# The router before the experts: last attention slab by token halves, logits as a plain f32 product of transposed x, choice on unscaled logits, first expert begun on half of its rows

## The reference, cut to what matters

```python
x = x + memory_cross_attention(rms_norm(x, xa_norm_g[i]), mem_n, xa_wq[i], xa_wkv[i], xa_wo[i])
h = rms_norm(x, ffn_norm_g[i])
...
logits = (t @ router_w).astype(jnp.float32)          # t = h, (256, 1024); router_w (1024, 8)
top_v, top_i = lax.top_k(logits, TOP_K)              # 2 of 8
top_w = jax.nn.softmax(top_v, axis=-1)
gates = jnp.sum(jax.nn.one_hot(top_i, N_EXPERTS) * top_w[..., None], axis=1)
for e in range(N_EXPERTS):
    out = out + gates[:, e:e + 1] * swiglu(t, w_gate[e], w_up[e], w_down[e])
```

## Time and profile before

| | us |
|---|---|
| median of 3 runs | 1642.45 |
| lowest and highest | 1641.81, 1644.15 |
| the profiled execution | 1642.63 |
| its span, first to last instruction | 1640.7 |

### The profile page before, as it was taken

The page is one execution under the profiler, slowest core; times in us unless marked ns, Lnnn a source line. Parts: engine busy times, 40 slices in busy tenths (PEclk is TensorE's granted clock), DMA queues, the critical chain, the costliest instruction groups (busy, mean ns, idle before and its releaser), DMA issues.

```text
span 1640.7 us, 22659 instructions
## 1 busy us (share of the span) xinstructions
PE 1614.0 (98%) x8508; PEld 1378.6 (84%) x8508; DVE 1271.0 (77%) x1070; ACT 1036.0 (63%) x908; POOL 55.5 (3%) x52
## 2 busy tenths in 40 slices
PE   7999999999999999999999999999999999999997
PEld 6998989998887798888788888888888888888885
DVE  7776646454567675799888888888888888889897
ACT  5443445544356544677777777777777777777775
POOL 1000000000000101100000000000000000000010
PEclk9999999999999999999999999999999999999999
DMA  9644535555554354899999999999979999999994
GB/s 355 206 155 154 160 123 180 180 182 199 161 192 140 129 217 174 286 377 356 371 389 371 384 384 372 377 390 370 383 289 357 383 390 368 392 371 369 382 395 162
DMA packets 226030, 474.71 MB, mean 289 GB/s; under 512 B 7698, under 2 KB 52964, under 8 KB 225972
## 3 DMA queue, kind: packets, MB, share of 16 engines
q1 hardware_dynamic: 221552, 459.01, 77.7%
q0 software_dynamic: 3104, 10.66, 1.9%
q10 hardware_dynamic: 1316, 4.24, 0.6%
HBM read 466.01 MB, written 7.87 MB: 289 GB/s over the span
## 4 chain that ended last, share of the span: by engine, by line
PE 88%; issue 5%; DVE 3%; ACT 2%; DMA 1%; POOL 1%; ACTq 0%; POOLq 0%; SPq 0%; DVEq 0%
PE ps L2313 34%; PE ps L2336 16%; PE ps L1845 15%; PE ps L1811 9%; PE ps L1831 4%; PE ps L2074 4%; PE ps L2321 1%; DVE w_lo L393 1%; ACT w_hi L389 1%; PE ps L1986 1%; PE ps L2006 1%; DMA ta<-xn,rden 1%; DMA raw<-in_ev_w_in 0%; PE ps L2100 0%; PE ps L1940 0%
## 5 line engine op out<-in xcount | busy, mean ns | idle before, releaser
L393 DVE TENSOR_TENSOR w_lo<-raw,w_hi 128x2048 fp32r<-128x2048 f32 x430 | 980.0, 2291 | 223.7 <-ACT w_hi L389 222.5
L389 ACT ACTIVATE w_hi<-raw 128x2048 fp32r<-128x2048 f32 x430 | 823.6, 1918 | 296.7 <-PE ps L2313 110.9
L2313 PE MATMUL ps<-w_hi,e_hi 128*128 128x512 f32 x896 | 355.6, 397 | 1.0 <-DVE w_lo L393 0.8
L2313 PE MATMUL ps<-w_hi,e_lo 128*128 128x512 f32 x896 | 349.8, 390 | 0.0
L2313 PE MATMUL ps<-w_lo,e_hi 128*128 128x512 f32 x896 | 349.3, 390 | 0.0
L2313 PEld LDWEIGHTS ps<-w_hi,e_hi 128*128 128x128 f32 x896 | 168.4, 188 | 38.5 <-DVE w_lo L393 3.2
L2313 PEld LDWEIGHTS ps<-w_hi,e_lo 128*128 128x128 f32 x896 | 168.2, 188 | 36.0
L2313 PEld LDWEIGHTS ps<-w_lo,e_hi 128*128 128x128 f32 x896 | 168.5, 188 | 33.1
L2336 PE MATMUL ps<-w_hi,at_hi 128*128 128x512 f32 x448 | 175.9, 393 | 0.4 <-DVE w_lo L393 0.4
L2336 PE MATMUL ps<-w_hi,at_lo 128*128 128x512 f32 x448 | 174.6, 390 | 0.0
L2336 PE MATMUL ps<-w_lo,at_hi 128*128 128x512 f32 x448 | 174.5, 390 | 0.0
(11 more groups left out here) (359 smaller groups left out, 1717.1 us busy)
## 6 DMA issues: line engine op xcount, KB each, us to landing
raw<-in_moe_w_up SPq DMA_DIRECT2D x112, 1024.0 KB, 7.9
raw<-in_moe_w_gate SPq DMA_DIRECT2D x110, 1024.0 KB, 7.5
raw<-in_moe_w_down SPq DMA_DIRECT2D x110, 1024.0 KB, 7.2
raw<-in_xa_wkv SPq DMA_DIRECT2D x16, 1024.0 KB, 5.2
raw<-in_ev_w_in SPq DMA_DIRECT2D x14, 1024.0 KB, 9.5
raw<-in_od_w_in SPq DMA_DIRECT2D x12, 1024.0 KB, 5.1
raw<-in_ffd_w_gate SPq DMA_DIRECT2D x11, 1024.0 KB, 5.4
raw<-in_ffd_w_up SPq DMA_DIRECT2D x11, 1024.0 KB, 5.3
```

What stands on the lines that cost most here:

```text
L389: nc.scalar.activation(w_hi[:, n % CUT, :], at_, ACT.Copy).then_inc(hi_cut, 1)
L393: nc.vector.tensor_tensor(w_lo[:, n % CUT, :], place(n, r, behind)[0], w_hi[:, n % CUT, :].bitcast(F32), ALU.subtract).then_inc(lo_cut, 1)
L2313: mm = T.matmul(ps[:, bank, :], s, m, start=(h == 0 and k == 0 and j == 0), stop=(h == 1 and k == 3 and j == 2))
```

## The change

- The fourth `o1` slab runs its four k for token half 0 first and then for token half 1, where it took both in each k. `o_top` tells that half 0 is complete; DVE adds each token half by itself. Transposes of X and parts of the logits stand between the slab's matmuls.
- The router's matrix is multiplied with the gain once (`router_g`), and the logits are a plain f32 product with the transposed x (`xt`, plain copies by ACT and DVE) as the stationary operand and 8 columns of `router_g` moving: they come out as tokens by 8. `r_hi`, `r_lo`, the block `logits`, its turning back and the scaling are gone.
- The choice reads the unscaled logits out of `ps`; only the difference of the two largest is scaled with `rstd`, for the softmax. The squares come scaled by 1/1024, and their last sum is made on POOL.
- `upto` (= `before` + `ident`) in place of `before` counts a token itself too, so that `pack` follows from the product with one step between. The counts of all tokens go to another bank and are waited for later.
- `keep_going` gives 25 transposes in place of 60.
- `cut_hi` of slab G0+2 stands behind the scaling of `ta`; Exp and the load of the Silu table stand behind `rows_hi`; the stores of POOL wait until the gather is done.
- `opening` waits for the first half of `e_lo` ahead of its first slab and for the second ahead of its second.

```diff
@@ POOL, ahead of the root
                     for h in range(2):
-                        pool.wait_ge(acc_free, BANKS["o1"] + 2 * h + 2)
                         half_ = slice(512 * h, 512 * h + 512)
                         for t in range(2):
+                            pool.wait_ge(acc_free, BANKS["o1"] + (2 if h == 0 else 3 + t))
                             nc.gpsimd.tensor_tensor(tat[:, t, half_], X[:, t, half_], g_row[:, half_],
                                                     ALU.mult).then_inc(xg_mul, 1)
+                    pool.wait_ge(n_var, k + 1)
+                    pool.wait_ge(n_sq, 2 * [n for n in NORMS if n != "ret"].index("moe") + 4)
+                    nc.gpsimd.tensor_tensor(var[:, 0:2], var0[:, :], sums[:, 2:4], ALU.add).then_inc(pool_link, 1)
+                    pool.wait_ge(pool_link, 1 + 1)
                 root(k, 16 if name == "ret" else 2)
                 if name == "moe":
                     pool.wait_ge(n_out, 2 * (NORMS["moe"] + 1))
+                    pool.wait_ge(e_ps, 2)
@@ ACT
             cut_hi(act, G0 + 1)
-            for h in range(2):
-                act.wait_ge(acc_free, BANKS["o1"] + 2 * h + 2)
-                turn_hi("moe", a_hi, tiles=range(4 * h, 4 * h + 4))
...
-            cut_hi(act, G0 + 2)
+            nc.scalar.activation(mx[:, 0:1], ident[:, 0:1], ACT.Copy).then_inc(g_sig, 1)
+            part_squares(0, 0)
+            part_squares(0, 1)
+            for b in range(2):
+                act.wait_ge(xt_ps, b + 1)
+                nc.scalar.activation(xt[:, 2 * b:2 * b + 2, :], pair(4 + b), ACT.Copy).then_inc(xt_a, 1)
+            for t in range(2):
+                act.wait_ge(xt_ps, 3 + 2 * t)
+                nc.scalar.activation(xt[:, 4:6, t * P:(t + 1) * P], pair(6)[:, :, t * P:(t + 1) * P],
+                                     ACT.Copy).then_inc(xt_a, 1)
+                part_squares(1, t)
@@ DVE
             cut_lo(dve, G0 + 1)
...
             V.memset(ones[:, :], 1.0)
+            V.tensor_tensor(upto[:, :], before, ident, ALU.add)
+            link(V.tensor_scalar(rank, e8, -1.0, float(NE), ALU.mult, ALU.add))
+
+            for t in range(2):
+                if t == 0:
+                    dve.wait_ge(o_top, 1)
+                else:
+                    dve.wait_ge(slab_used, FIRST["o1"] + 4)
+                freed(V.tensor_tensor(X[:, t, 512:1024], acc("o1", 1, 2)[:, t, :], X[:, t, 512:1024], ALU.add), 1)
+                if t == 0:
+                    dve.wait_ge(n_sq, 2 * [n for n in NORMS if n != "ret"].index("moe") + 2)
+                    V.tensor_scalar(var0[:, :], sums[:, 0:2], EPS, None, ALU.add).then_inc(n_var, 1)
+                dve.wait_ge(xt_ps, 4 + 2 * t)
+                V.tensor_copy(xt[:, 6:8, t * P:(t + 1) * P], pair(7)[:, :, t * P:(t + 1) * P]).then_inc(xt_v, 1)
             dve.wait_ge(r_lt, 1)
@@ DVE, behind the counts
-            dve.wait_ge(r_ps, 2)
+            dve.wait_ge(c_ps, 2)
             cps = ps[:, 1, 0:16].rearrange("p (t e) -> p t e", t=2)

             link(V.tensor_tensor(first, cps, mask, ALU.mult))
-            link(V.tensor_tensor(first, first, mask, ALU.add))
-            link(V.tensor_scalar(pos16[:, :, 0:NE], first, -1.0, None, ALU.add))
+            for t in range(2):
+                ins = V.tensor_scalar(pack[:, t, :], slot, 1.0, first[:, t, 0:1], ALU.add, ALU.is_equal)
+            ins.then_inc(packed, 1)
@@ PE
+            def logit_part(t, h):
+
+                pe.wait_ge(r_w, 1)
+                pe.wait_ge(xt_a, 2 if h == 0 else 3 + t)
+                if h == 1:
+                    pe.wait_ge(xt_v, 1 + t)
+                for k in range(4 * h, 4 * h + 4):
+                    mm = T.matmul(ps[:, LOGITS + t, 0:NE], xt[:, k, t * P:(t + 1) * P],
+                                  router_g[:, NE * k:NE * k + NE], start=k == 0, stop=k == KT - 1)
@@ PE, the fourth slab of o1
+                    for t in range(2):
+                        for k in range(4):
+                            pe.wait_ge(xs_lo, XH * i + 2 + k // 2 + 1)
+                            if (t, k) == (0, 3):
+                                turn_x(0, (0, 1))
+                            if (t, k) == (1, 2):
+                                turn_x(1, (0,))
+                            if (t, k) == (1, 3):
+                                logit_part(0, 0)
+                            ah, al = (a[:, 4 + k, t * P:(t + 1) * P] for a in (a_hi, a_lo))
+                            for j, (s, m) in enumerate(cuts(ah, al, wh[:, k, :], wl[:, k, :])):
+                                mm = T.matmul(ps[:, (c + t) % 4, :], s, m, start=False, stop=(k == 3 and j == 2))
@@ PE, behind the slab
+            logit_part(1, 0)
+            turn_x(1, (1,))
+            logit_part(0, 1)
+            logit_part(1, 1)
...
+            keep_going(22)
             pe.wait_ge(r_cnt, 1)
```

More of the change, by code:

```diff
@@ L805, in _ @@
             od_cut(5)
-            act.wait_ge(in_router, 16)
-            act.wait_ge(r_z, 1)
-            nc.scalar.activation(r_hi[:, 0:KT * NE], router[:, :], ACT.Copy).then_inc(r_w, 1)
             od_copy("oq1", 2)
@@ L915, in _ @@
             rows_hi(0)
+            act.wait_ge(r_m, 1)
+            nc.scalar.activation(lg[:, 9, 2:4], lg[:, 9, 0:2], ACT.Exp).then_inc(r_e, 1)
+            nc.scalar.activation(mx[:, 0:1], ident[:, 0:1], ACT.Silu)
             for n in range(3, 6):
@@ L1570, in rows_lo @@
                     dve.wait_ge(row_h, 2 * k + j + 1)
-                    ins = V.tensor_tensor(e_lo[:, 4 * j:4 * j + 4, :], shaped(ps[:, 6 + j, :], 4),
-                                          e_hi[:, 4 * j:4 * j + 4, :].bitcast(F32), ALU.subtract)
-                ins.then_inc(e_l, 1)
+                    V.tensor_tensor(e_lo[:, 4 * j:4 * j + 4, :], shaped(ps[:, 6 + j, :], 4),
+                                    e_hi[:, 4 * j:4 * j + 4, :].bitcast(F32), ALU.subtract).then_inc(e_l, 1)
             rows_lo(0)
@@ L2243, in _ @@
             cross(1, xa_q1, xa_k1, xa_v1, xa_pt1)
[L2247 to L2257 removed]
+            logit_part(1, 0)
+            turn_x(1, (1,))
+            logit_part(0, 1)
+            logit_part(1, 1)
             def keep_going(n):
                 for _ in range(n):
[L2261 to L2268 removed]
+                    T.transpose(ps[:, 4, 0:P], ident, ident)
+            keep_going(22)
             pe.wait_ge(r_cnt, 1)
             mask = lg[:, 8, :]
[L2271 to L2272 removed]
+            T.matmul(ps[:, 1, 0:8], upto[:, :], mask[:, 0:8], start=True, stop=True)
+            T.matmul(ps[:, 1, 8:16], upto[:, :], mask[:, 8:16], start=True, stop=False)
             T.matmul(ps[:, 1, 8:16], ones[:, :], mask[:, 0:8], start=False, stop=True).then_inc(c_ps, 2)
[L2274 to L2277 removed]
+            T.matmul(ps[:, 5, 0:8], ones[:, :], mask[:, 0:8], start=True, stop=False)
+            T.matmul(ps[:, 5, 0:8], ones[:, :], mask[:, 8:16], start=False, stop=True).then_inc(r_ps, 1)
+            keep_going(3)
             def gather(k):
```

113 lines of the change are left out of this document (47 added, 66 removed).

## The result

The changed kernel takes 1666.97 us (median of 4 runs, 1662.70 to 1670.62) against 1642.44 us (1641.81 to 1644.15) for the kernel before: ratio 1.0145, 95% interval 1.0131 to 1.0158. The forecast was 1639.9 us, so the kernel became 24.5 us slower where 2.6 us of gain were expected. The profiled execution took 1666.67 us, 1664.8 of them span. The four runs line up by their mean granted clock: 1662.70 us at 0.997, 1666.67 at 0.995, 1667.27 at 0.994 and 1670.62 at 0.992. The profiled run of the kernel before had 0.998.

A forecast was written before the change was run, and what follows sets the result against it. PE was taken as busy nearly throughout, so only the 17.8 us from last slab to opening could pay. A 0.44 us loss within a 1.3 us earlier gather led to a 2.6 us earlier opening: 1639.9 us, range 1638.5 to 1641.4.

The forecast's parts named there:

- the last sentence of the first part: Behind the first expert's opening at 672.31: PE streams at 0.2275 us a matmul, so an earlier opening moves everything after equally.
- the rivals: Four alternative outcomes: choice not held (0.24), arms later (0.17), weights give it back (0.06), slower by the clock (0.04).
- slower: the clock: At the opening: TensorE falls to 1.2 GHz, its 48 matmuls taking up to 10.9 us more, 1650.8 us; chance 0.04.
- The slab: Last attention slab: PE waits some 2.4 us for DVE's add, with `upto` held behind POOL's multiply; add ends at 655.55.
- not held: Last slab: `upto` and the choice are not held, stall 1.3 us, gain 3.7 to 4.1 us; chance 0.24.
- Logits, choice, counts, gather: Behind the slab: logits read at 661.66, choice done 663.94, counts 665.03, gather starts 665.87, 1.3 us gained.
- the arm over `e_lo`: Before the opening: cuts and `e_lo` on DVE end at 669.4, the gather at 669.44, opening at 669.7.
- What costs nothing: Behind the gather: moved Exp, table load, stores and weight loads stay hidden, as do dropped fillers and the router's edits near 485.
- paced by PE: After 770: the first reader of `xn` comes at a place paced by PE, so the later stores cost nothing.
- The sum: Whole kernel: opening 2.6 us earlier, giving 1639.9 us, -0.16%; the forecast's own band 1639.2 to 1640.4 has chance 0.49.
- The local terms: Last slab to opening: slab and logits lose 0.44 us, gather starts 1.3 us earlier, opening 2.6 us earlier.

The follow-up runs named there:

- e2: Kernel before the change, with unused `table` columns cut from 24 to 16, so tensors behind it begin 32 bytes lower: 1665.15 us, ratio 1.0138.
- e12: Changed kernel in its own order, only `var0` grown to 256 bytes (`[P, 64]`): 1644.71 us over 11 runs, ratio 1.0005.
- e4: Changed kernel with 64-byte `var0`; DVE does half 0's add and `var0` before the cut, `ones`, `upto`, `rank` last: 1661.17 us, ratio 1.0117.
- e3: Changed kernel with 64-byte `var0` and `upto` moved behind the last copy of `xt`: 1668.70 us, ratio 1.0156.
- e10: Changed kernel with e4's DVE order and `var0` of 256 bytes (`[P, 64]`): 1638.14 us over 11 runs, ratio 0.9975.
- e13: e10 with 12 products of 512 columns in place of the 22 filler transposes: 1637.49 us over 5 runs, ratio 0.9964.
- e9: Changed kernel with e4's order, 64 unused bytes ahead of everything and `var0` of `[P, 192]`: 1638.24 us, ratio 0.9977.
- e11: Changed kernel in its own order, `var0` of `[P, 64]`, ten unused 512-column products where PE stood in the last slab: 1638.92 us, ratio 0.9981.
- e8: e5 with 20 unused transposes ahead of token half 0's transposes in the last slab: 1663.68 us, ratio 1.0120.
- e14: e10 with 64 unused bytes between `w_lo` and `X`, and `var0` of `[P, 48]`: 1639.47 us, ratio 0.9979.
- e5: Changed kernel in its own order, only `var0` grown to 128 bytes (`[P, 32]`): 1665.79 us, ratio 1.0139.

## Why the prediction was wrong

**The step that failed** is the last sentence of the first part: "Behind 672.31 PE streams at 0.2275 us a matmul, so an earlier opening should move all that follows by as much". It took the pitch of 0.2275 us as a property of the product. It depends on where the operands lie: records of 390 ns where the distance between stationary and moving tensor is a multiple of 256 bytes, 395 ns otherwise, at the same granted clock. The change broke that for every tensor behind `var0`, and none of the rivals held it, since each looked at what the instructions do and in which order. That `logits` goes and `var0` comes was known; that 1024 bytes go out and 8 come in was passed over. Price: 22.9 us by e2 alone; 1666.97 less the 1644.71 of e12 is 22.3 us. Of the loss 20.2 us lie behind the opening. The 2.4 us ahead of the slab fit the products on `m_hi`, `od_hi` and `f_hi`, which show the same 5 ns (`w_lo,m_hi` has 390 ns at L1811 of the kernel before and 395 at L1827 of the changed one). There are 552 of them, and at 6 ns each from start to start they cost 3.3 us; the 384 products with `m_hi` or `m_lo` moving give 1.2 us back at 3 ns each. That is an estimate of 2.2 us.

**The second error is the price and chance of the clock.** The rival "slower: the clock" got 0.04 and a place at the opening. In the changed kernel's order the clock is halved for long in nine runs of eleven (e12, by their mean clock), ahead of the opening, over the small products and fillers: this costs some 5.7 us. In the changed kernel's own profile it is 25.53 us from the slab's start to the opening, less 2.34 of wait and the 18.88 of e4, which is 4.3 us. The evidence against it, 2.03 us busy of 4.00 from 780, was of a stretch between full slabs and told nothing about a stretch of small products and transposes.

**The slab.** Right, and by its own arithmetic. The forecast was a wait from 653.18 to 655.60, 2.42 us long; measured 2.34 us (655.62, by the pitch, to 657.96). `upto` takes its turn behind POOL's multiply (1.21 us against 0.27 or 0.28 alone). The Trainium skill (SBUF — State Buffer, "SBUF: two separate sides") has the exclusive lock on the shared port pair, and here the trace agrees also for an operation 16 times smaller than a cut. By these runs the rival "not held" fell. What I didn't see is that taking `upto` away would not help: `rank` is held in its place (e3, 1.09 us). The remedy is to put the add ahead of the whole group (e4).

**Logits, choice, counts, gather.** In e4, without wait and half clock, the slab's start to the read of the logits takes 11.10 us (650.60 to 661.70); the forecast's 13.45 less the wait of 2.42 is 11.03. From the read to the gather 4.22 us, forecast 4.21. From the gather to the opening 3.56 us, forecast 3.83: the arm over `e_lo` was not late. These terms hold within 0.3 us.

**What costs nothing.** Right for the weights and the table load: with the distances mended the time from the opening to the end of the span is 966.2 us in e10 (1637.8 - 671.57), against 968.4 before. But the first reader of `xn` wasn't "paced by PE", as the prediction has it. The stretch from 780 of the earlier trace rows is PE's wait for those rows, 1.97 us until 782.29, in the kernel before and, shorter or longer, in the others; the wait in the list of PE's waits from 672 on, before and in e13:

```profile
PE ps L2301 <- DMA ta<-xn,rden: 2.0, 1, 2.0
```

```profile
PE ps L2339 <- DMA ta<-xn,rden: 2.7, 1, 2.7
```

It is 1.5 us in the changed kernel, 0.3 in e10 and e12, 0.5 in e9 and 1.6 in e11. So most of the 2.2 us gained behind the opening in e10 is this wait, which the forecast had no term for. What sets it wasn't tried.

**The sum.** With the place mended and no long half-clock stretch, the changed order takes 1639.2 us (the two runs of e12), against 1639.9 forecast. The local terms were priced well, each measured within 0.3 us. That the whole also meets the forecast within 1 us is in part luck, since the wait for `xn` and the 0.6 us by which the slab starts later in e12's profile (648.85 against 648.21) were no terms of it. What it missed are two effects that the edits touch, worth 22 and 5.7 us.

**Left open.** Why a distance of 256 bytes matters is not known; only the rule for these fp32 products was seen, and only for rests of 0, 32, 64, 128 and 224. What lets the clock fall isn't settled either. Standing isn't needed (e8, e10), but it goes with the long stretches: a mean granted clock of 0.994 or less has nine of eleven runs of e12, none of the 30 of e9, e10 and e14, where the add comes first, and none of the ten of e11, where large products fill the wait. Twelve large products in the fillers' place (e13) may help further, which five runs can't tell, and two profiles of one order can differ (e9 none, e10 10.2 us).

## What to carry to other kernels

A change in the size of a small tensor moves all tensors behind it. Compare the addresses of the large operands before and after, above all the distance between stationary and moving tensors, and pad so that it stays; look at the mean record of the largest product groups before reading any wait. When a loss is larger than the edited stretch, cut the span at the edit's start and end first: here that showed in one step that 22.7 of 24.1 us lay outside it. And an operation that another engine waits for doesn't belong behind small preparations that can be held by GpSimd, however cheap these are alone.

## What the runs showed of the hardware that was not expected

- 512-column products of fp32r tensors: mean record 389 to 391 ns where stationary and moving tensor lie a multiple of 256 bytes apart, 394 to 396 ns at rests of 32, 64, 128 and 224 (`w_lo` groups); with 4032 such products 20 us. With 256 columns it is the other way round and smaller: 283 ns at rests of 0 and 128, 281 at 224, 279 or 280 at 32 and 64.
- A one-source DVE operation of 16 columns is held by a GpSimd multiply as a two-source one is: 1.09 us (e3) against 0.16 where the multiply was over (the changed kernel).
- Half-clock stretches of 3.4, 10.2, 13.7 and 20.5 us within a program whose PE is otherwise busy, each beginning between the last products of the last attention slab and the fillers behind it, with and without a wait of PE ahead of it; the longest (e5) lasts almost to the end of the gather. Four f32 products of 8 columns (8 records) take 0.95 us at 2.4 GHz and 1.71 us at 1.2 GHz.
